# Twelve sublayers of a three-term fp32 transformer on one core: how modulation rows are fetched and summed, and who rounds the second opening block

## The reference, cut to what matters

```python
cond = silu(c)
for i in range(4):                                  # layers, 3 sublayers each
    mod = (cond @ w_mod[i] + b_mod[i]).reshape(-1, 3, 3, 1024)   # shift, scale, gate per sublayer
    x = sublayer(x, swiglu_0, mod[:, 0], 0.5)
    x = sublayer(x, mla | diff_attn | mamba2 (i % 3), mod[:, 1], 1.0)
    x = sublayer(x, swiglu_1, mod[:, 2], 0.5)
# sublayer: y = f(x * (1 + scale) + shift); layernorm(alpha * x + weight * gate * y, g, b)
# then a second block: rms_norm, hybrid mixer, cross attention, swiglu on the same 256 x 1024 x
```

## Time and profile before

| | us |
|---|---|
| median of 3 runs | 3261.58 |
| lowest, highest | 3259.24, 3275.2 |
| the profiled execution, its own time | 3266.8 |
| span of its instructions | 3264.9 |
| PE busy | 2814.4 (86%) |
| DVE busy | 1961.0 (60%) |
| POOL busy | 1336.1 (41%) |
| ACT busy | 1203.6 (37%) |
| granted TensorE clock, mean | 0.893 of full |
| HBM read | 573.20 MB, 176 GB/s |

### The profile page before, as it was taken

The page is one execution under the profiler, slowest core; times in us unless marked ns, Lnnn a source line. Parts: engine busy times, 40 slices in busy tenths (PEclk is TensorE's granted clock), DMA queues, the critical chain, the costliest instruction groups (busy, mean ns, idle before and its releaser), DMA issues.

```text
span 3264.9 us, 50689 instructions
## 1 busy us (share of the span) xinstructions
PE 2814.4 (86%) x20791; PEld 2694.3 (83%) x20791; DVE 1961.0 (60%) x2306; ACT 1203.6 (37%) x1335; POOL 1336.1 (41%) x1170
## 2 busy tenths in 40 slices
PE   3998779989976899898879889989878988869797
PEld 3997679989974899898774789989868988569797
DVE  5656666566548665665666566565576554664553
ACT  2433334334333343333332334343344434234442
POOL 1872947367293573672930067277191000000000
PEclk9998979989887898998885889899888998779898
DMA  7764547557472574673640357376454554124453
GB/s 268 266 230 142 189 154 248 202 200 248 145 251 84 172 252 168 223 250 138 232 144 0 110 200 248 132 260 242 136 174 145 185 191 131 51 79 141 130 184 111
DMA packets 357166, 576.16 MB, mean 176 GB/s; under 512 B 22255, under 2 KB 297898, under 8 KB 356906
## 3 DMA queue, kind: packets, MB, share of 16 engines
q1 hardware_dynamic: 357034, 574.29, 51.9%
HBM read 573.20 MB, written 1.05 MB: 176 GB/s over the span
## 4 chain that ended last, share of the span: by engine, by line
PE 66%; DVE 16%; issue 6%; DMA 5%; ACT 4%; POOL 2%; SPq 1%; DVEq 0%; POOLq 0%; ACTq 0%
PE ps L1587 56%; DMA raw<-in_ffn_w_in_dram 3%; ACT whi L654 3%; PE ps L1689 2%; DVE wlo L1004 2%; PE ps L1950 1%; DVE z L1116 1%; PE ps L1941 1%; POOL mod_acc L639 1%; DVE prob L1277 1%; DVE conv L1405 1%; DVE acc L1122 1%; DVE ax L1038 1%; PE ps L1770 1%; DVE stat L1261 1%
## 5 line engine op out<-in xcount | busy, mean ns | idle before, releaser
L1004 DVE TENSOR_TENSOR wlo<-raw,whi 128x2048 fp32r<-128x2048 f32 (+1 forms) x402 | 1020.4, 2541 | 756.5 <-ACT whi L654 752.8
L1587 PE MATMUL ps<-H_hi,whi 128*128 128x256 f32 x4256 | 1240.0, 291 | 143.9 <-DVE am L1213 62.2
L1587 PE MATMUL ps<-H_lo,whi 128*128 128x256 f32 x4256 | 1231.8, 289 | 0.0
L1587 PE MATMUL ps<-H_hi,wlo 128*128 128x256 f32 x4256 | 1230.1, 289 | 0.0
L654 ACT ACTIVATE whi<-raw 128x2048 fp32r<-128x2048 f32 (+1 forms) x402 | 759.4, 1891 | 729.1 <-DMA raw<-in_ffn_w_in_dram 300.0
L1587 PEld LDWEIGHTS ps<-H_hi,whi 128*128 128x128 f32 x4256 | 846.8, 199 | 153.9 <-issue 65.8
L1587 PEld LDWEIGHTS ps<-H_lo,whi 128*128 128x128 f32 x4256 | 846.8, 199 | 0.1
L1587 PEld LDWEIGHTS ps<-H_hi,wlo 128*128 128x128 f32 x4256 | 845.5, 199 | 0.0
L639 POOL TENSOR_TENSOR mod_acc<-mod_acc,mod_w 128x512 f32<-128x512 f32 x462 | 730.6, 1608 | 0.0
L1587 PE MATMUL ps<-A_hi,whi 128*128 (+1 forms) x1880 | 536.8, 286 | 18.2 <-DVE wlo L1004 18.2
L1587 PE MATMUL ps<-A_hi,wlo 128*128 (+1 forms) x1880 | 535.5, 285 | 0.0
(11 more groups left out here) (291 smaller groups left out, 2286.8 us busy)
## 6 DMA issues: line engine op xcount, KB each, us to landing
raw<-in_ffn_w_in_dram SPq DMA_DIRECT2D x176, 1024.0 KB, 5.2
mod_w<-in_w_mod_dram SPq DMA_DIRECT2D x180, 768.0 KB, 6.5
raw<-in_ffn_w_out_dram SPq DMA_DIRECT2D x88, 1024.0 KB, 4.9
raw<-in_w_gate_up_dram SPq DMA_DIRECT2D x22, 1024.0 KB, 5.0
raw<-in_ssm_w_in_dram SPq DMA_DIRECT2D x20, 1024.0 KB, 6.5
raw<-in_w_in_dram SPq DMA_DIRECT2D x14, 1024.0 KB, 5.1
raw<-in_diff_w_in_dram SPq DMA_DIRECT2D x12, 1024.0 KB, 7.1
raw<-in_w_down_dram SPq DMA_DIRECT2D x11, 1024.0 KB, 4.8
```

The source lines that it names most:

```text
L1004: tt(wlo[b % RAW][:, r], raw[b % RAW][:, r], whi[b % RAW][:, r].bitcast(F32), ALU.subtract).then_inc(w_lo, 1)
L1587: m = pe.matmul(out, l, r, start=first and i == 0, stop=last and i == 2, skip_group_check=rest)
```

## The change

1. **Where units stand in SP's queue.** ffn: after blocks 5, 6, 8, 10 ... 27 in place of 2, 4, 6 ... 28. ssm and diff: the first after block 4 in place of 2 and 3. mla: a new order, below. `mod_used` is split into one semaphore for each half, so a load waits for its own half.
2. **mla.** DVE does five of the 16 units (k = 0 to 4 of half 0) in one instruction each, between its own work; POOL does the other 11.
3. **The sum over partitions.** At the end of `projected` ACT copies mod_acc to mod_hi (128x3072, fp32r), DVE writes mod_lo = mod_acc - mod_hi. PE, in `ending` after column 1, waits for mod_lo and adds both into six rows of one bank with 12 matmuls of 512 columns and 6 stationary columns; ACT copies the six rows out of PSUM; after column 3 PE turns them with 4 transposes. The 24 matmuls of `mod_sums` leave ln (they stay in init).
4. **The second opening block.** Its rounding moves from the end of `projected` into ln: ACT's after z's columns 0 and 1, DVE's low part, now its first half alone, after column 3. POOL does the second half in two pieces of 512. In ln `sqsum` moves forward, to stand right behind `zsum`.
5. **The opening.** PE waits for the first half of the low part alone; in row k it takes both terms with H_hi first (waiting for H_hi only) and the one with H_lo after. The second half is waited for at k = 4.

```diff
-    if kind == "mla":
-        turns = [1, 1, 5, 6, 7, 8, 10] + 9 * [12]
-    elif kind == "diff":
-        turns = [1, 1] + [3 + 5 * j // 4 for j in range(8)] + 6 * [15]
-    elif kind == "ssm":
-        turns = [1, 1] + [2 + 3 * j // 2 for j in range(14)]
+        order = [(0, 0), (0, 1), (1, 0), (1, 1), (2, 0), (3, 0), (2, 1), (4, 0), (3, 1), (4, 1), (5, 1), (6, 1), (7, 1), (5, 0), (6, 0), (7, 0)]
+        turns = [1, 1, 3, 5, 5, 6, 7, 8, 8, 10] + 6 * [12]
     else:
-        turns = [1, 1] + [2 + 2 * j for j in range(14)]
+        order = [(k, half) for k in range(DC) for half in range(2)]
+        pace = {"diff": [4 + 5 * j // 4 for j in range(7)] + 7 * [15], "ssm": [4 + 3 * j // 2 for j in range(14)],
+                "ffn": [5 + 7 * j // 4 for j in range(14)]}
+        turns = [1, 1] + pace[kind]
...
-                sp.wait_ge(mod_used, u - 1)
+                sp.wait_ge(mod_used[half], DC * sub + k)
...
+            def second_half(st):
...
+                pool.wait_ge(w_hi, b + 1)
+                pool.wait_ge(w_lo, b)
+                for i in range(2):
+                    r = slice(HALF + 512 * i, HALF + 512 * i + 512)
+                    low = nc.gpsimd.tensor_tensor(wlo[b % RAW][:, r], raw[b % RAW][:, r], whi[b % RAW][:, r].bitcast(F32), ALU.subtract)
+                low.then_inc(w_lo, 1)
...
# ACT, end of projected; DVE has its like with mod_lo
+                after = steps[steps.index(st) + 1]
+                if after.kind == "ln":
+                    sub = after.args[0] + 1
+                    for half in range(2):
+                        act.wait_ge(mod_used[half], DC * (sub + 1))
+                    copy(mod_hi[st.kind][:, :, :], mod_acc[:, :, :]).then_inc(s["mod_hi"], 1)
...
# ACT, ln
+                    if c == 2:
+                        if st.kind == "ln":
+                            act.wait_ge(s["mod_row"], n["mod_row"] + 1)
+                            copy(mod_row[0:6, :], ps[0:6, 7, :]).then_inc(s["mod_turn"], 1)
+                        g = steps[steps.index(st) - 1].lin["out"]
+                        convert(g.b + g.n + 1)
...
# DVE, ln
-                gated(0), gated(1), zsum(1)
-                gated(2), gated(3), zsum(2), zsum(3), sqsum(1)
-                gated(4), gated(5), zsum(4), zsum(5), sqsum(2), sqsum(3)
-                gated(6), zsum(6), sqsum(4), sqsum(5), sqsum(6)
+                gated(0), gated(1), zsum(1), sqsum(1)
+                gated(2), gated(3), zsum(2), zsum(3), sqsum(2), sqsum(3)
+                convert_open(st, 0)
+                gated(4), gated(5), zsum(4), zsum(5), sqsum(4), sqsum(5)
+                gated(6), zsum(6), sqsum(6)
...
# PE, ending
+                        if c == 1 and after.kind == "ln":
+                            pe.wait_ge(s["mod_lo"], after.n["mod_lo"] + 1)
+                            for j in range(6):
+                                r = slice(j % 3 * 512, j % 3 * 512 + 512)
+                                for x in (mod_hi[st.kind], mod_lo):
+                                    m = pe.matmul(ps[0:6, 7, :], pick[:, 5 - j:11 - j], x[:, j // 3, r], start=j == 0 and x is not mod_lo,
+                                                  stop=j == 5 and x is mod_lo)
+                            m.then_inc(s["mod_row"], 1)
+                        if c == 3 and after.kind == "ln":
+                            pe.wait_ge(s["mod_turn"], after.n["mod_turn"] + 1)
+                            for j in range(4):
+                                m = pe.transpose(ps[:, 7, 8 * j:8 * j + 6], mod_row[0:6, j * P:j * P + P], ident[0:6, 0:6])
+                            m.then_inc(s["mod_sum"], 1)
```

More of the change, by code:

```diff
@@ L90, in constants @@
     c["misc"][:, 4] = 1.0
+    c["pick"] = np.zeros((P, 11))
+    c["pick"][:, 5] = 1.0
     first = list(c)
@@ L227, in __init__ @@
         self.free = [0, 0]
-        parts = 0
+        parts = opens = 0
         for name, *args in steps:
@@ L231, in __init__ @@
             parts = SIGNALS[name].get("h_lo", parts)
+            opens += name in ("ffn", "mla", "diff", "ssm", "hyb", "xatt")
+            st.opens = opens
             st.parts = parts
@@ L394, in program @@
         acc = at("acc", [P, 3, S], room(12 * S))
+        mod_lo = at("mod_lo", [P, 2, MODU], o_acc, F32R)
+        mod_hi = {"ffn": at("mod_hi", [P, 2, MODU], o_hh, F32R), "mla": at("mod_hi_att", [P, 2, MODU], o_ah, F32R)}
+        mod_hi["ssm"], mod_hi["diff"] = mod_hi["ffn"], mod_hi["mla"]
+        mod_row = at("mod_row", [P, 512], o_s1)
         pool_tick = at("pool_tick", [P, 16], room(64))
@@ new lines, in _ @@
+            done = [0]
+            pool.wait_ge(s["cond_ready"], 1)
+            for st in steps:
+                if "out" in st.lin and (st.kind in ("hyb", "xatt") or st.args[0] + 1 >= SUB * DEPTH):
+                    second_half(st)
+                if st.kind not in ("ffn", "mla", "diff", "ssm") or st.args[0] + 1 >= SUB * DEPTH:
+                    continue
+                sub = st.args[0] + 1
+                pool.wait_ge(s["mod_sum"], sub)
+                pool.wait_ge(s["ax_ready"], sub)
+                if st.kind == "mla":
+                    for k in range(DC):
+                        modulate(sub, k, 1)
+                    for k in range(MLA_DVE, DC):
+                        modulate(sub, k, 0)
+                else:
@@ L640, in _ @@
-                            added.then_inc(mod_used, 1)
+                            modulate(sub, k, half)
+                second_half(st)
         @block.scalar
@@ L1235, in projected @@
                 g = st.lin["out"]
-                walk(dve, g, lambda i, it: convert(g.b + i + 2, it), 1, 2)
+                walk(dve, g, lambda i, it: None if it is None and i == g.n - 1 else convert(g.b + i + 2, it), 1, 2)
+                after = steps[steps.index(st) + 1]
+                if after.kind == "ln":
+                    dve.wait_ge(s["mod_hi"], after.n["mod_hi"] + 1)
+                    tt(mod_lo[:, :, :], mod_acc[:, :, :], mod_hi[st.kind][:, :, :].bitcast(F32), ALU.subtract).then_inc(s["mod_lo"], 1)
             def attend(n, heads, scale, kind):
@@ L1567, in dve_post @@
                     tt(ax[:, r, :], ax[:, r, :], z[:, r, :], ALU.add).then_inc(s["ax_ready"], 1)
+            opened = {next(iter(st.lin.values())).b + 2 for st in steps if st.lin}
             tri3 = kc("tri")
@@ L1629, in opening @@
                     wait_banks(g.p + i)
-                    wait_split(g.b + i, 0)
+                wait_split(g.b, 0)
+                pe.wait_ge(w_open, st.opens)
                 for k in range(DC):
+                    pe.wait_ge(s["h_hi"], st.n["h_hi"] - st.parts + k * st.parts // DC + 1)
+                    if k == DC // 2:
+                        wait_split(g.b + 1, 0)
+                    for i in range(2):
+                        for c in range(2):
+                            r = slice(k * 256 + c * P, k * 256 + c * P + P)
+                            for w in (whi, wlo):
+                                pe.matmul(ps[:, bank(g.p + i) + c, 0:S], w[(g.b + i) % RAW][:, r], H_hi[:, k, :],
+                                          start=k == 0 and w is whi, stop=False)
                     whole(st, k)
@@ L1634, in opening @@
                         for c in range(2):
-                            m = three(ps[:, bank(g.p + i) + c, 0:S], (g.b + i) % RAW, k * 256 + c * P, P, H_hi[:, k, :], H_lo[:, k, :],
-                                      k == 0, k == 7)
+                            r = slice(k * 256 + c * P, k * 256 + c * P + P)
+                            m = pe.matmul(ps[:, bank(g.p + i) + c, 0:S], whi[(g.b + i) % RAW][:, r], H_lo[:, k, :], start=False, stop=k == DC - 1)
                             if k == DC - 1:
@@ L1706, in pe_init @@
                 m.then_inc(s["vec_turned"], 1)
-                pe.wait_ge(mod_used, 16)
+                for half in range(2):
+                    pe.wait_ge(mod_used[half], DC)
                 pe.wait_ge(s["z_in"], 1)
-                mod_sums(0, 16)
-                mod_sums(16, 24)
+                pe.wait_ge(s["picked"], 1)
+                mod_sums()
             def folded(n, signal):
```

139 lines of the change are left out of this document (84 added, 55 removed).

## The result

| | before | after |
|---|---|---|
| median of the runs, us | 3265.96 (4 runs) | 3236.32 (4 runs) |
| lowest and highest | 3259.24, 3275.2 | 3234.97, 3237.77 |
| span of the profiled execution, us | 3264.9 | 3235.2 |
| forecast, us | | 3170, range 3139 to 3220 |

The change is faster by 0.87%: a ratio of 0.9913, 95% interval 0.9892 to 0.9933. The forecast was 92 us of gain, the chip gives 30. The direction was right, and the time lies 16 us above the range.

The account below looks back on a forecast made before the run. PE was taken to set the ffn pace, with pauses from queued modulation loads and stage boundaries on top. Terms of -83, -1, -5 and -3 sum to -92: 3174.8 us for this execution, 3170 against the median, range 3139 to 3220.

Parts of the forecast that it names:

- Part 1: SP's queue in ffn, ssm and diff: later modulation units free the blocks and remove PE's pauses, minus 83 us.
- Part 2: Both mla stages: fewer POOL units at the end gain 7.6 and 5.4, DVE's five units cost 12, sum minus 1 us.
- Part 3: Stage boundaries: wide matmuls pause PE 4.6 us in the ending but shorten the layernorm, minus 0.5 each, minus 5 for eleven.
- Part 4: Second opening block's rounding moved into the norms: last layernorm gains 4.5, two rms norms lose 1.7 each, sum minus 3 us.
- The check that POOL keeps up: In ffn stages, POOL's 8.7 us a unit fits the tighter pace of 10.1, so no term was added.
- In the open 18 for both stages: Upper bound on DVE's five mla units, 1.82 us each, 9.1 a stage; 12 was taken.
- mla stages longer by more than 9: One of the signs listed as showing the forecast wrong; the size is in us.
- (c): Rival: POOL's two pieces hold DVE's layernorm sums, 3.2 us for each of 14 stages, 45 us: 3215; chance 0.08.
- (a): Rival: the pause in the ending costs more, each of eleven boundaries loses 3 us, 38 more: 3208; chance 0.12.
- (b): Rival: the clock is kept over the ending's 4.6 us pause, each boundary gains 3 us: 3142; chance 0.10.
- (d): Rival: DVE low parts in ffn caught behind POOL's run, 20 such events cost 150 us: 3320; chance 0.04 with its like.
- (e): Rival: the new order does not free SP's queue, half of the queue-order gain stays: 3212; chance 0.06.

Follow-up runs that it names:

- Experiment 1: The kernel before with only the new queue turns of the modulation loads for ffn, ssm and diff: 3173.99 us, ratio 0.9723.
- Experiment 3: The changed kernel with POOL's last six units of each mla stage taken from the two halves in turn: 3208.83 us, ratio 0.9826.
- experiment 4: The changed kernel with all sixteen mla units on POOL in the old order, none on DVE: 3202.45 us, ratio 0.9809.
- experiment 5: Experiment 3's kernel with the loads of mla units (4,0) and (3,1) moved behind the first out block in SyncE's queue: 3205.80 us, ratio 0.9812.
- experiment 9: Second half of the opening block's low part on DVE instead of POOL: 3230.25 us in the changed kernel, 3113.81 us in the kernel of 8.
- kernel of 8: The changed kernel with the modulation sum rounded one block earlier in all stages and mla units dealt three to DVE, thirteen to POOL, halves in turn: 3132.26 us.
- experiment 7: The changed kernel with mod_hi and mod_lo rounded one block earlier in every stage but mla: 3193.42 us, ratio 0.978.
- experiment 2: The changed kernel with the old queue turns of the modulation loads put back for ffn, ssm and diff: 3348.02 us, ratio 1.0239.
- experiment 6: The changed kernel with three mla units on DVE, thirteen on POOL, halves in turn, out blocks ahead of DVE-dependent loads: 3194.38 us, ratio 0.9769.

## Why the prediction was right or wrong

Experiment 1 splits the change. By the profiled spans the new order takes 95.8 (3264.9 to 3169.1), and the rest adds 66.1 (3169.1 to 3235.2). By place, from first matmul to next first, change against experiment 1:

| | forecast | measured |
|---|---|---|
| Part 1, order | -83 | -95.8 in spans, -90.5 in medians |
| Part 2, mla (with its share of Part 3) | -2 | +50.7 (25.0 and 25.7) |
| Part 3, wide sums, the nine other stages with modulation | -4 | +8.0 |
| Part 4, from ffn11 to the end | -3 | +5.9 |
| start of the first stage | 0 | +1.5 |

**Part 1 was right in mechanism and 8 to 13 too small.** The six ffn stages gave 12.3 each (11 forecast, bounds 9.5 and 12.4): the low part of block 3, which was to be late next, was not. (The 205.3 of the forecast is the mean of the two stages shown; all six have 204.9.) ssm gave 16.5 (10), the first ffn stage 2.9, for which I had nothing. diff gave 0.7 (7): the pause went, but DVE was then last at its boundary. I had priced the pause and not asked who would be last in its place. The check that POOL keeps up went wrong without cost: I held its unit at 8.7 us against a pace of 10.1. At the new pace the same units keep POOL busy for 148 us a stage in place of 126 (windows of ffn2), about 10 us for each of the fourteen, and it hardly stands between them any more, where it stood 3 us before most of them. In ffn2 of experiment 1 it ends 29.5 us before the stage does, so nothing waits for it; but there is no margin left.

**Part 2 is the step that failed**, and it is most of the miss: 53 of the 62 us between forecast and result. The step reads: "With 11 units left to POOL and six behind the last block this goes: 7.6 here; for the second mla stage I take 5.4, so minus 13." I counted POOL's units and not the order in which they use the two buffers, though the diff shows three of one half and then three of the other. Experiment 3 shows that order to cost 15.6 a stage. I also held the work that the wide sums put into `ending` (Part 3) against the ffn stages alone, where POOL is done early. In mla POOL is the last engine, and PE waits for mod_lo with its whole ending behind it: experiment 4, where only that is left, stands at 157.3 against 153.7. So the 25.3 us a stage are 15.6 for the order of the halves, 6.1 for DVE's five units with what waits behind them (experiment 3 against 4), and 3.6 for the wide sums. Third, "In the open 18 for both stages" bounded DVE's five units by their own length. A unit of DVE's is also a release for SyncE, and a weight block stood behind that load: 15.92 for a unit of 1.82; experiment 5 takes 11 off this pause, and 5 of them come back one head later. The wrong sign that I gave as a mark ("mla stages longer by more than 9") was the right place to look.

**Part 3 was right event by event, with a sum 1.4 too low in an ffn stage** (0.9 longer, 0.5 less was forecast). The pause 4.47 (4.6), mod_lo 3.36 (3.4), spread after 4.24 us (4.4), the opening 2.5 after the spread (2.4). From column 1 to PE's end 18.0 was measured and 18.4 drawn. What was missed lies on DVE: its last z comes 20.1 after column 1, not 19, since GpSimd's pieces fall among its sums. That is rival (c) below its price: against 3.2 us a stage, experiment 9 shows 1.2 (an ffn stage with its boundary took 211.3 on the mean without them, 212.5 with them). The ending's pause, which I took as given by the change's shape, was an order that could be turned (experiment 7), and it held 43 us.

The Trainium skill, Trainium Architecture — The Big Picture, What this means for kernel authors, calls what DVE and GpSimd share an exclusive lock and not a split of bandwidth. The trace agrees: DVE's low part does not run at half speed beside POOL, it stands for a whole unit (8.06 less its own 2.29 is 5.8, a unit's 5.9) or for one addition (last section), and the tick at 1549.01 stands 2.24 for DVE.

**Part 4** was small and wrong in sign. ffn11's boundary gave 2.2 (4.5 forecast), but hyb and xatt lost 3.2 and 3.4, of which 1.9 each lie in the norm's boundary (21.0 to 22.9; 1.7 forecast); the opening by H_hi, from which I took 0.7 each off, gives nothing that can be seen there. Experiment 9 shortens these boundaries by 0.9 (22.9 to 22.0), and the weight matmuls of the hyb stage then take 1.5 longer. The remaining 1.5 lie behind xatt's end. Where they come from, and the 1.3 and 1.5 inside hyb and xatt, stays open.

**The rivals.** None reached the time. (a), the pause in the ending costs more (3208), is right that the pause is dearer, but by its place in mla, not by the ffn boundaries. (c), GpSimd's pieces (3215), is nearest in time and a small part of the cause: taken out they give 6 us here and 8 to 18 in the kernel of 8, not 45. (b) did not happen: the clock fell to half behind a pause of 4.5. (d), the starved low parts, did not happen in the change, but did in experiment 2 for 19.68, in 6 for 8.06 twice and in 9 for 8.07. (e) is refuted by experiment 1. No rival named mla as a loss of its own: the range took 3 us for each boundary and had none for 25.

## What to carry to other kernels

Before moving units between engines, write down for each buffer who fills it and who frees it, in order: two buffers only overlap if consecutive units use different ones, and a load that waits for an engine holds every load behind it in the queue. Price a step that moves into the critical engine's stream in every stage where it runs, above all where its producer is the last engine. And time the cheapest part of a change alone: here three lists of numbers held more than the whole of it, and the rest paid only after two orders were turned (3132.3 in place of 3236.3; 3106.7 with two pieces of the work taken off GpSimd as well).

## What the runs showed of the hardware that was not expected

A VectorE low part (two SBUF inputs, 128x2048, 2.29 us alone) that starts within 0.02 us behind a GpSimd unit's tick can stand for the whole unit, 8.06 us (twice in experiment 6, 8.07 once in experiment 9), and once for three units, 19.68 us, until GpSimd ran out of work. It need not: of twelve such starts in the fourteen traces these four were long, and eight took 2.32 to 2.34. Of 138 that started 0.02 to 0.06 behind a tick one was long. Seven more, begun at or within 0.33 us of a unit's first product, took 6.48 to 7.13. Beside an addition it is regular: all 63 low parts that started in the first 0.06 us of one took 3.36 to 3.48, the wait for that one addition (1.29) and no more. The long waits come and go with edits elsewhere: the ssm stage took 340.8 to 353.9 us in five kernels that are alike there (the change and experiments 3 to 6, with the same instructions in that stage). A difference of 10 us between two such kernels has to be checked against these events before it is explained.

Around a pause of PE of 4.5 us the granted clock was half for the first eight matmuls behind it, 0.42 apart, and full (0.24) from the ninth on.
